# One core, two-layer hybrid decoder step: paired gate products, the first tile's output projection moved behind the prompt's scan, decay products moved to GpSimd

## The chip, the cores and the metric

One NeuronCore of a Trainium2 chip runs the whole step as one program. The metric is device time in microseconds (us); the time of a kernel is the median over its runs. A trace of one profiled execution gives the rest.

## The reference, cut to what matters

256 prompt tokens and 64 sample tokens (8 sequences of 8) go through a Mamba-2 mixer, a PEER mixer (each token fetches 128 rows of an expert table), then an attention layer and a second PEER. The change lies in the Mamba mixer and the first PEER's selection:

```python
zxbcdt = u @ w_in                      # z: gate, xbc: conv input, dt
xbc = silu(conv(xbc)); dt = softplus(dt + dt_bias); a = -exp(a_log)
# scan, chunks of 128 tokens (prompt: 2 chunks), sample: one chunk of 8 tokens in each sequence
cum = cumsum(dt * a);  decay = exp(cum_t - cum_s) for s <= t
y = (C B^T * decay) @ xdt + (C @ h) * exp(cum)
h = h * exp(cum_last) + B^T @ (tail * xdt)
y = (y + d_skip * xs) * silu(z);  y = group_rmsnorm(y) * norm_g;  h_res += y @ w_out
# PEER: q = rmsnorm(h_res) @ w_query; top 16 of 128 for each half key, top 16 of the 256 sums,
# out = sum_k gate_k * gelu(x . U[idx_k]) * V[idx_k]
```

## The kernel before, in words

Tokens lie in three tiles: tiles 0 and 1 are the prompt (128 rows each), tile 2 the samples (64 rows). All data are float32. Every engine runs one program written out in order; they meet at semaphores. PSUM has eight banks that TensorE claims round robin: `claim` waits until the bank's last reader has freed it. Weights come through a ring of four 1 MB slots (`wring`) filled by SyncE's queue in the order of `loads`; a slot is refilled when the last product that uses it is through.

The stages, in order:

1. **Gate (z).** `project_block("z", n, KD)`, four blocks of 512 columns, each in two halves of four chunks of 128; for every tile 4 matmuls of 512 columns a half (line 588). In float32 each matmul leaves two records in the trace (two passes). ScalarE makes the tanh, VectorE the rest of silu.
2. **xbc and convolution.** 32 blocks of 128 channels (line 630); VectorE does the convolution.
3. **Prompt scan.** Steps n = 0 to 15: 8 groups for tile 0, then 8 for tile 1. `decays(n)` on VectorE multiplies a mask by `da` (line 1970, 128x512), TensorE makes the segment sums from it (line 678) and C B^T (line 681), ScalarE the exp (line 1482), VectorE masks it (`mix`, lines 1983 and 1986), TensorE multiplies by xdt (line 701) and makes the new state (line 708). VectorE adds up y and gates it (lines 2132 to 2159). GpSimd makes xdt, its tailed copy and the skip term (lines 2526, 2527, 2529), two steps behind `gated`. After step 7 and step 15 the tile's rows are normalised (`scale_rows`, line 1995) and turned (`turn_rows`).
4. **Sample scan.** Steps g = 0 to 7 (n = 16 to 23). In each, TensorE turns 16 blocks of old state (`sample_turn`, line 560), makes the next step's segment sums, y, the state's part (line 659, 32 records: eight sequences times two halves of the output partitions, alternating) and the state update (line 667: four matmuls with 64 rows of contraction each, `rows = slice(64 * q, 64 * q + 64)`, 8 records). GpSimd scales the old states (line 2543, 128x1024, twice a step), VectorE adds the update (line 2103). Between these, `after_sample_turn(g)` puts the first tile's next work: output projection in two blocks (g = 0 and 1, line 588 again), norm for PEER (g = 2), queries (g = 2 to 5, line 746), scores (line 731), and on VectorE the first ten of twenty selection steps of tile 0 (`early_picks`, 3, 3, 2, 2 at g = 4 to 7; a quad of heads has five steps).
5. **Gathers.** When VectorE says `scan_over` (line 1883 after `turn_rows(2)`), GpSimd starts the expert gathers (line 2564), 1280 of 512 KB each in seven phases; VectorE multiplies every gathered `peer_u` row by the token (`dot`, line 2220), TensorE sums the `peer_v` rows (line 1103). Everything else (selection of later tiles, late output projection of tiles 1 and 2, attention) runs beside the gathers.

Of the kernel before, what the change touches and what calls it, by code (L numbers as in the profile page):

```python
# [36 lines left out]
ARENA = 31744  # L37


C_ID, C_TRI, C_STRICT, C_TRIS, C_STRICTS, C_ONES, C_BM, C_ID2, C_IOTA, C_END = 0, 128, 256, 384, 448, 512, 640, 648, 712, 728  # L40


def shape_constants():
# [12 lines left out]
    c[64:, C_BM:C_BM + 4] = k // DEC_T == 4 + np.arange(4)[None, :]  # L56
# [75 lines left out]
def build(nc, I, O, counts):  # L132
# [3 lines left out]
    with ctx:  # L136
# [123 lines left out]

        load_sent = [0]

        def load_weights(sp, upto):
            while load_sent[0] < upto:
                i = load_sent[0]
                if i >= NW:
                    sp.wait_ge(*full_at(last_user[i - NW]))
                sp.dma_start(slot_view(i), loads[i][0]).then_inc(*w_ready[i % NW].mark(by=16))
                load_sent[0] += 1
# [284 lines left out]
        def _(pe):  # L554
# [38 lines left out]
            def project(key, nblocks, kchunks):  # L593
                for n in range(nblocks):
                    project_block(key, n, kchunks)
# [11 lines left out]
            project_block("z", 0, KD)  # L607
# [6 lines left out]
            for n in range(1, 4):  # L614
                project_block("z", n, KD)
# [33 lines left out]
            def sample_states(g):  # L649
# [21 lines left out]
            def scan_front(t, g):  # L671
# [3 lines left out]
                pe.wait_ge(*dve_done.at(("seg", t, g)))  # L675
# [115 lines left out]
            for n in range(3 * GROUPS):  # L791
# [327 lines left out]
            def late():  # L1119
# [4 lines left out]
                for n in range(2):  # L1124
                    acc = {t: claim(pe, ("late_out", n, t)) for t in (1, 2)}
                    for part in range(4):
                        w = weight(pe, ("late_out", n, part), ("late_out", n, 2))
                        for t in (1, 2):
# [4 lines left out]
                            if part == 3:  # L1133
                                mm.then_inc(*full(("late_out", n, t)))
                        yield
# [23 lines left out]
            def first_select():  # L1159
                for _ in range(10):  # L1160
                    yield
# [61 lines left out]
        def _(sp):  # L1223
# [58 lines left out]
            load_state(3)  # L1282
            for g in (6, 7):
                store_final(g)
            for g in range(8):
# [4 lines left out]
                if g < 6:  # L1290
                    load_weights(sp, load_index[("out", 0, 0)] + (8, 10, 14, 16, 18, 20)[g])
# [108 lines left out]
        def _(act):  # L1400
# [28 lines left out]
            for n in range(4):  # L1429
                for t in range(3):  # L1430
                    bank = filled(act, ("z", n, t))
                    s(act.activation(z[0:ROWS[t], t, n * 512:(n + 1) * 512], bank[0:ROWS[t], :], ACT.Tanh, scale=0.5),
                      act_done, ("ztanh", n, t))
# [67 lines left out]
            def after_sample_turn(g):  # L1501

                if g == 0:
                    take_sub_keys(0)
                if g == 1:
                    square("ffn0", 0, dve_done.at(("h", "mix", 0, 0)))
                if g == 2:
                    take_turned("ffn0", 0)
                if 2 <= g < 6:
                    for b in range(4 * g - 8, 4 * g - 4):  # L1510
                        bank = filled(act, ("q", b))
                        freeing(act.activation(qT[:, b, 0:128], bank[:, 0:128], ACT.Copy), ("q", b))
                if g in (3, 4, 6):
                    take_score(0, 0, (0, 1, None, 2)[g - 3])
# [310 lines left out]
            def first_select():  # L1825
                for _ in range(10):
# [51 lines left out]
        def _(dve):  # L1878
# [47 lines left out]
            for n in range(4):  # L1926
                for t in range(3):
# [4 lines left out]
                    freeing(dve.tensor_tensor(zz, zz, bank[0:ROWS[t], :], ALU.mult), ("z", n, t))  # L1932
# [143 lines left out]
            def after_sample_turn(g):  # L2076

                if g < 2:
                    add_to_h("out", 0, 0, g)
                if g == 1:  # L2080
                    norm("ffn0", FFN_SLOT, (0,))
                if g >= 4:
                    advance(early_picks, (3, 3, 2, 2)[g - 4])

            def block_rows(g):

                if g >= 2:
                    dve.wait_ge(*full_at(("hupd", 2 * g - 3, 1)))
                s(dve.tensor_tensor(bm[:, g % 2, :, :], repeat(btok[:, 2, g * 128:(g + 1) * 128], 4),
                                    spread(cst[:, C_BM:C_BM + 4], 128), ALU.mult), dve_done, ("bm", g))  # L2090
# [16 lines left out]
            def first_picks():  # L2107
                for q in range(2):
# [3 lines left out]
            decays(0)  # L2112
# [487 lines left out]
```

## Time and profile before

| | us |
|---|---|
| median of 3 runs (2558.26 to 2571.83) | 2562.1 |
| the profiled execution's own time | 2563.79 |
| its span in the trace | 2562.0 |
| TensorE busy (70%) | 1794.2 |
| VectorE busy (61%) | 1575.0 |
| GpSimd busy (52%) | 1324.9 |
| ScalarE busy (12%) | 305.0 |

859 MB move in all, 671 MB of them by the gathers. A share of busy time is a mean over stages with different limits. The stages are read from the windows of the trace, and in a stage the wait that ends last tells what limits it. Times of one instruction on GpSimd are rough.

### The profile page before, as it was taken

To read this page: it belongs to the slowest core of one execution; us is meant where nothing else is said; L and a number is where in the kernel's file an instruction comes from. 1 tells how busy PE (TensorE), PEld (TensorE's weight loads), DVE (VectorE), ACT (ScalarE), POOL (GpSimd) and SP (SyncE) were. 2 spreads that over 40 slices of the span, in tenths; PEclk is the share of its full clock that TensorE was granted. 3 is DMA by queue.
4 is the path that set the end of the run, shared out by engine and by line. 5 is a ranking of instruction groups with operands and counts; after the bars stand their busy time and mean duration, and the time that the engine had idled before them with its cause. 6 is when DMAs were issued, how large, how long until landed. Compare 5 with 4: busy or idle time off the path is not lost.

```text
span 2562.0 us, 23629 instructions
## 1 busy us (share of the span) xinstructions
PE 1794.2 (70%) x7688; PEld 800.3 (31%) x7688; DVE 1575.0 (61%) x3823; ACT 305.0 (12%) x705; POOL 1324.9 (52%) x1480
## 2 busy tenths in 40 slices
PE   7999888676405666668778576776665658456678
PEld 4477756524400010022334223351123422001112
DVE  2288875999798656652644988768764353833321
ACT  2133322201000000010101011110012110000000
POOL 0011443255547777755665445754555363577774
PEclk9999899887756666788899786787777778699999
DMA  4232228599989999999999999999999999999997
GB/s 154 99 104 95 90 80 282 165 357 386 403 293 388 409 409 409 409 395 402 384 407 401 402 401 358 407 400 400 399 374 349 320 378 374 388 409 410 409 408 305
DMA packets 325848, 859.13 MB, mean 335 GB/s; under 512 B 26841, under 2 KB 93353, under 8 KB 325697
## 3 DMA queue, kind: packets, MB, share of 16 engines
q0 software_dynamic: 184320, 671.17, 66.7%
q1 hardware_dynamic: 141406, 186.46, 21.0%
q8 instruction: 62, 1.02, 0.2%
q14 instruction: 60, 0.49, 0.1%
HBM read 845.25 MB, written 12.17 MB: 335 GB/s over the span
## 4 chain that ended last, share of the span: by engine, by line
DMA 23%; POOL 18%; PE 12%; issue 8%; DVE 5%; SPq 3%; ACT 0%; POOLq 0%; DVEq 0%; ACTq 0%
POOL arena L2564 18%; DMA arena<-peer_v,arena 10%; DMA wring<-w_q 5%; PE banks L896 4%; PE banks L1103 3%; DMA wring<-cache_v 2%; DVE arena L2220 2%; DMA arena<-peer_u,arena 2%; SPq L1336 2%; DMA wring<-w_kv 1%; PE banks L1012 1%; SPq L1334 1%; DMA wring<-ple_w_gate 1%; DMA wring<-peer_w_query 1%; PE banks L560 1%
## 5 line engine op out<-in xcount | busy, mean ns | idle before, releaser
L2220 DVE SCALAR_TENSOR_TENSOR arena<-arena,banks 128x1024 f32<-128x1024 f32 x640 | 762.3, 1219 | 441.5 <-DMA arena<-peer_u,arena 435.7
L1103 PE MATMUL banks<-arena 128*32 128x512 f32 x2560 | 692.9, 718 | 351.6 <-DMA arena<-peer_v,arena 344.6
L2564 POOL DMA_INDIRECT arena<-peer_v,arena x640 | 607.8, 950 | 416.7 <-PE banks L1103 179.8
L2564 POOL DMA_INDIRECT arena<-peer_u,arena x640 | 606.8, 948 | 412.3 <-issue 188.7
L1103 PEld LDWEIGHTS banks<-arena 128*32 128x32 f32 x2560 | 92.5, 116 | 823.5 <-DMA arena<-peer_v,arena 655.2
L896 PE MATMUL banks<-wring,uT 128*128 128x512 f32 (+3 forms) x448 | 224.2, 650 | 67.5 <-DMA wring<-w_q 28.0
L560 PE MATMUL banks<-cst,arena 128*128 128x128 f32 (+6 forms) x498 | 78.0, 305 | 163.1 <-DVE arena L2236 83.4
L896 PEld LDWEIGHTS banks<-wring,uT 128*128 128x128 f32 (+1 forms) x448 | 80.2, 189 | 219.0 <-issue 168.1
L630 PE MATMUL banks<-uT,wring 128*128 128x320 f32 x512 | 139.1, 433 | 0.0
L560 PEld LDWEIGHTS banks<-cst,arena 128*128 128x128 f32 (+6 forms) x498 | 60.5, 156 | 213.8 <-DVE arena L2236 83.6
L588 PE MATMUL banks<-wring,uT 128*128 128x512 f32 (+1 forms) x256 | 115.8, 609 | 0.6 <-DVE arena L2103 0.6
L630 PEld LDWEIGHTS banks<-uT,wring 128*128 128x128 f32 x512 | 96.7, 190 | 40.2 <-issue 0.8
L2511 POOL COPY arena<-arena 128x3 f32<-128x3 f32 x32 | 6.0, 186 | 186.8 <-ACT arena L1458 186.8
L560 PE MATMUL banks<-cst,u 128*128 128x128 f32 (+1 forms) x256 | 43.2, 331 | 52.6 <-DVE u L1904 47.3
L834 PE MATMUL banks<-uT,wring 128*128 128x128 f32 x512 | 69.2, 293 | 9.6 <-issue 9.6
L834 PEld LDWEIGHTS banks<-uT,wring 128*128 128x128 f32 x512 | 63.9, 204 | 34.8 <-issue 34.8
L1131 PE MATMUL banks<-wring,uT 128*64 128x512 f32 (+1 forms) x128 | 62.2, 639 | 16.3 <-DMA wring<-ssm_w_out 11.9
L2027 DVE MAX8 arena<-arena 128x8 f32<-128x128 f32 (+1 forms) x208 | 60.6, 333 | 17.3 <-ACT arena L1495 16.4
L2030 DVE FIND_INDEX8 arena<-arena 128x8 uint32<-128x128 f32 (+1 forms) x208 | 67.4, 336 | 0.0
L588 PEld LDWEIGHTS banks<-wring,uT 128*128 128x128 f32 (+1 forms) x256 | 44.7, 180 | 69.4 <-issue 68.5
L2271 DVE TENSOR_SCALAR arena<-arena 128x512 f32<-128x512 f32 (+1 forms) x10 | 4.4, 437 | 92.6 <-ACT arena L1634 92.6
L560 PEld LDWEIGHTS banks<-cst,u 128*128 128x128 f32 (+1 forms) x256 | 35.6, 180 | 78.8 <-DVE u L1904 41.7
(265 smaller groups left out, 1941.6 us busy)
## 6 DMA issues: line engine op xcount, KB each, us to landing
wring<-peer_w_query SPq DMA_DIRECT2D x40, 1024.0 KB, 17.1
wring<-ssm_w_in SPq DMA_DIRECT2D x24, 1024.0 KB, 7.3
wring<-w_q SPq DMA_DIRECT2D x18, 1024.0 KB, 21.0
wring<-ssm_w_out SPq DMA_DIRECT2D x16, 1024.0 KB, 9.3
wring<-ple_w_gate SPq DMA_DIRECT2D x12, 1024.0 KB, 12.6
arena<-peer_u,arena POOLq DMA_INDIRECT x640, 12.0
arena<-peer_v,arena POOLq DMA_INDIRECT x640, 12.4
out_sample_ssm<-arena SPq DMA_DIRECT2D x16, 512.0 KB, 5.6
```

Of the source, the lines that this page charges most:

```text
L560: mm = pe.transpose(bank[0:c, col:col + r], src, ident[0:r, 0:r])
L588: mm = pe.matmul(acc[t][0:ROWS[t], 0:w.shape[2]], uT[:, kk, OFF[t]:OFF[t] + ROWS[t]], w[:, k, :], start=(kk == 0), stop=(kk == kchunks - 1))
L630: mm = pe.matmul(acc[:, 0:NTOK], w[k // 4][:, k % 4, j * 128:(j + 1) * 128], uT[:, k, :], start=(k == 0), stop=(k == KD - 1))
L834: mm = pe.matmul(bank[:, 0:R], w[k // 4][:, k % 4, (b % 4) * 128:(b % 4 + 1) * 128], uT[:, k, OFF[t]:OFF[t] + R], start=(k == 0), stop=(k ...
L896: mm = pe.matmul(bank[0:ROWS[t], 0:w.shape[2]], uT[:, kk, OFF[t]:OFF[t] + ROWS[t]], w[:, k, :], start=(kk == 0), stop=(kk == kchunks - 1))
L1103: mm = pe.matmul(sums(t, at, half), place_of(t, at), rows_buf[:, k, half * 512:(half + 1) * 512], start=at < spots(t), stop=False, skip_gr ...
L1131: mm = pe.matmul(acc[t][0:ROWS[t], :], uT[:, kk, OFF[t]:OFF[t] + ROWS[t]], w[:, k, :], start=(kk == 0), stop=(kk == 15))
L1336: sp.dma_start(last, rows[PAST - 128:, 0:2, :].rearrange("m h d -> m (h d)")).then_inc(*ready.mark(p, by=16))
L2027: step(j, dve.max(out_v[:, o], values))
L2030: step(j, dve.max_index(out_i[:, o], out_v[:, o], values))
L2220: dve.scalar_tensor_tensor(rows_buf[:, k, :], rows_buf[:, k, :], 1.0, u_now, ALU.mult, ALU.mult, accum_out=pact[:, n % 2, at:at + 1]).then ...
L2564: pool.indirect_dma_start(rows_buf[:, k, :], None, tables[kind], bass.IndirectOffsetOnAxis(ap=rows, axis=0))\
```

## The change

- **Halved gate.** For tile 2 the 512 columns of a gate block are made as two matmuls of 256 columns, whose outputs lie in the two partition halves of one bank. ScalarE and VectorE read the bank in two pieces.
- **Narrow state update.** The four matmuls of line 667 contract over 32 rows each, on four different groups of 32 rows (the four sequences that each of them needs); the mask `bm` changes to match.
- **First tile's output projection.** Its two blocks go behind step 15's scan (block 0) and into g = 0 (block 1); norm, queries, scores and selection steps all come one sample step earlier, selection has twelve early steps (3, 3, 2, 2, 2 from g = 3) and eight late ones instead of ten and ten. `part_read` frees a slot of the ring when one part of the projection has been read, for the late projection too. SyncE asks for block 1's weights before the last two stores of final prompt states.
- **Decays.** For tiles 0 and 1 the product of line 1970 is made by GpSimd, one step ahead, instead of by VectorE, two steps ahead. For tile 2 VectorE keeps it.

```diff
@@ tensor
+            def gate_block(n):
+
+                acc = {t: claim(pe, ("z", n, t)) for t in ALL}
+                for half in range(2):
+                    w = weight(pe, ("z", n, half), ("z", n, 2))
+                    for t in ALL:
+                        for k in range(4):
+                            kk = half * 4 + k
+                            for c in range(1 if t < 2 else 2):
+                                out, cols = (acc[t], w[:, k, :]) if t < 2 else \
+                                    (acc[t][64 * c:64 * c + 64, 0:256], w[:, k, 256 * c:256 * c + 256])
+                                mm = pe.matmul(out, uT[:, kk, OFF[t]:OFF[t] + ROWS[t]], cols, start=(kk == 0), stop=(kk == KD - 1))
...
-                        rows = slice(64 * q, 64 * q + 64)
+                        rows = slice(64 * i + 32 * q, 64 * i + 32 * q + 32)
...
-                pe.wait_ge(*dve_done.at(("seg", t, g)))
+                pe.wait_ge(*(pool_done if t < 2 else dve_done).at(("seg", t, g)))
...
+            def out_block(n):
+
+                bank = claim(pe, ("out", n, 0))
+                for part in range(4):
+                    pe.wait_ge(*freed(("yT", 0, part)))
+                    w = weight(pe, ("out", n, part), ("out", n, 0) if part == 3 else ("read", "out", n, part))
+                    for k in range(4):
+                        kk = part * 4 + k
+                        mm = pe.matmul(bank, uT[:, kk, 0:128], w[:, k, :], start=(kk == 0), stop=(kk == 15))
+                    mm.then_inc(*(full(("out", n, 0)) if part == 3 else part_read.mark(("read", "out", n, part))))
...
                 if g == 0:
                     turn_sub_keys(0)
-                    for q in range(4):
-                        pe.wait_ge(*freed(("yT", 0, q)))
-                if g < 2:
-                    project_block("out", g, 16, (0,))
-                if g == 2:
+                    out_block(1)
+                if g == 1:
                     pe.wait_ge(*freed(("sk", 0)))
                     norm_transposes("ffn0", (0,))
-                if 2 <= g < 6:
-                    first_queries(g - 2)
-                if g in (3, 4, 6):
-                    first_scores((0, 1, None, 2)[g - 3])
+                if 1 <= g < 5:
+                    first_queries(g - 1)
+                if g in (2, 3, 5):
+                    first_scores((0, 1, None, 2)[g - 2])
...
+                if n == 2 * GROUPS - 1:
+                    out_block(0)
@@ sync
+            load_weights(sp, load_index[("out", 0, 0)] + 8)
             for g in (6, 7):
                 store_final(g)
...
-                if g < 6:
-                    load_weights(sp, load_index[("out", 0, 0)] + (8, 10, 14, 16, 18, 20)[g])
+                if g < 5:
+                    load_weights(sp, load_index[("out", 0, 0)] + 12 + 2 * g)
@@ vector
-                if g < 2:
-                    add_to_h("out", 0, 0, g)
-                if g == 1:
+                if g == 0:
+                    add_to_h("out", 0, 0, 1)
                     norm("ffn0", FFN_SLOT, (0,))
-                if g >= 4:
-                    advance(early_picks, (3, 3, 2, 2)[g - 4])
+                if g >= 3:
+                    advance(early_picks, (3, 3, 2, 2, 2)[g - 3])
...
-            decays(0)
-            decays(1)
             mix(0)
             for n in range(3 * GROUPS):
...
-                if n + 2 < 3 * GROUPS:
+                if 2 * GROUPS <= n + 2 < 3 * GROUPS:
                     decays(n + 2)
...
+                if n == 2 * GROUPS:
+                    add_to_h("out", 0, 0, 0)
@@ gpsimd
+            decays(0)
+            decays(1)
             for n in range(3 * GROUPS):
                 t, g = divmod(n, GROUPS)
                 R, x = 128, n % 2
+                if 2 <= n + 1 < 2 * GROUPS:
+                    decays(n + 1)
                 pool.wait_ge(*freed(("cum", t)))
```

On TensorE, from the end of prompt step 15 (its last row is the turning of a final state, `cst,arena` x2) to sample step g = 1, before:

```order
L560 MATMUL banks<-cst,arena 128x128 x2
L560 MATMUL banks<-cst,u 128x128 x16
L678 MATMUL banks<-cst,arena 64x64 x4
L681 MATMUL banks<-arena 64x64
L701 MATMUL banks<-arena 64x64 x4
L659 MATMUL banks<-arena 64x128 x16
L667 MATMUL banks<-arena 128x512 x4
L560 MATMUL banks<-cst,arena 128x128 x20
L588 MATMUL banks<-wring,uT 128x512 x16
L560 MATMUL banks<-cst,arena 128x128 x16
```

and the same stretch of the changed kernel (its line 565 is the old 560, 779 the projection, 694 the old 678, 697 the old 681, 717 the old 701, 675 the old 659, 683 the old 667):

```order
L565 MATMUL banks<-cst,arena 128x128 x2
L779 MATMUL banks<-wring,uT 128x512 x16
L565 MATMUL banks<-cst,u 128x128 x16
L694 MATMUL banks<-cst,arena 64x64 x4
L697 MATMUL banks<-arena 64x64
L717 MATMUL banks<-arena 64x64 x4
L675 MATMUL banks<-arena 64x128 x16
L683 MATMUL banks<-arena 128x512 x4
L565 MATMUL banks<-cst,arena 128x128 x20
L779 MATMUL banks<-wring,uT 128x512 x16
L565 MATMUL banks<-cst,arena 128x128 x16
```

A whole projection block now stands between the end of the prompt's scan and the first turning of sample states, and the second block where the first was.

On GpSimd, the start of the prompt's scan, before (line 2526 makes xdt):

```order
L2526 TENSOR_TENSOR arena<-arena,small 128x256
L2527 TENSOR_TENSOR arena<-arena,small 128x256
L2529 TENSOR_TENSOR arena<-arena,small 128x256
L2526 TENSOR_TENSOR arena<-arena,small 128x256
L2527 TENSOR_TENSOR arena<-arena,small 128x256
```

and of the changed kernel (line 2554 is the decay product, 2572, 2573 and 2575 the three that were there):

```order
L2554 TENSOR_TENSOR arena<-cst,small 128x512 x2
L2572 TENSOR_TENSOR arena<-arena,small 128x256
L2573 TENSOR_TENSOR arena<-arena,small 128x256
L2575 TENSOR_TENSOR arena<-arena,small 128x256
L2554 TENSOR_TENSOR arena<-cst,small 128x512
L2572 TENSOR_TENSOR arena<-arena,small 128x256
```

Each prompt step gives GpSimd a fourth instruction, twice as wide as the others.

## Rows read from the trace of the kernel before

**Rows 1.** Windows by stage: us, busy us (count) of each engine, TensorE clock, DMA share, GB/s

```profile
28.00:118.00 90.00, 90.00 (x228) 34.95 (x227) 15.38 (x33) 10.98 (x19) 0.20 (x1) 1.00 0.20 71
118.00:270.00 152.00, 149.35 (x617) 108.11 (x617) 125.58 (x323) 50.99 (x124) 19.26 (x95) 1.00 0.28 97
...
444.00:516.00 72.00, 48.52 (x429) 40.61 (x429) 66.62 (x202) 15.37 (x36) 22.11 (x20) 0.82 0.52 166
516.00:760.00 244.00, 115.82 (x425) 72.97 (x423) 218.53 (x534) 14.38 (x44) 132.33 (x141) 0.73 0.98 371
760.00:2562.00 1802.00, 1232.46 (x4894) 418.69 (x4894) 1022.17 (x2467) 159.69 (x359) 1082.25 (x1139) 0.81 1.00 389
```

**Rows 2.** Timeline, gate stage, weight loads of TensorE (start us, us)

```profile
103.61 0.19 PEld L588 LDWEIGHTS banks<-wring,uT 128*64 128x64 f32 x2 [0.76 <-issue]
...
107.19 0.30 PEld L588 LDWEIGHTS banks<-wring,uT 128*128 128x128 f32 x2 [0.81 <-issue]
```

**Rows 3.** Timeline of TensorE, end of the prompt's scan and sample steps 0 and 1

```profile
346.43 1.91 PE L560 MATMUL banks<-cst,u 128*128 128x128 f32 x16
...
366.10 13.97 PE L588 MATMUL banks<-wring,uT 128*128 128x512 f32 x32 [0.61 <-DVE arena L2103]
379.90 1.91 PE L560 MATMUL banks<-cst,arena 128*128 128x128 f32 x16
...
383.32 1.97 PE L659 MATMUL banks<-arena 128*64 128x128 f32 x32
385.22 1.99 PE L667 MATMUL banks<-arena 64*128 64x512 f32 x8
387.14 13.14 PE L588 MATMUL banks<-wring,uT 128*128 128x512 f32 x30
```

**Rows 4.** Timeline of TensorE, sample steps 2, 3 and the start of 4

```profile
400.98 1.91 PE L560 MATMUL banks<-cst,u 128*128 128x128 f32 x16
...
413.80 7.38 PE L746 MATMUL banks<-uT,wring 128*128 128x128 f32 x64 [2.15 <-DVE arena L2148]
421.02 1.91 PE L560 MATMUL banks<-cst,arena 128*128 128x128 f32 x16
...
431.39 9.01 PE L746 MATMUL banks<-uT,wring 128*128 128x128 f32 x64 [2.64 <-issue]
...
441.13 1.91 PE L560 MATMUL banks<-cst,u 128*128 128x128 f32 x16
```

**Rows 5.** Timeline of VectorE, sample steps 4 to 7 and the end of the scan

```profile
444.01 0.22 DVE L1983 TENSOR_TENSOR arena<-banks,cst 64x64 f32<-64x64 f32 x1 [10.56 <-PE banks L681]
...
480.42 0.49 DVE L2027 MAX8 arena<-arena 128x8 f32<-128x128 f32 x2
...
482.90 0.22 DVE L1983 TENSOR_TENSOR arena<-banks,cst 64x64 f32<-64x64 f32 x1
...
489.59 0.49 DVE L2027 MAX8 arena<-arena 128x8 f32<-128x128 f32 x2
...
515.02 0.15 DVE L1883 COPY small<-cst 128x1 f32<-128x1 f32 x1
```

**Rows 6.** Timeline of VectorE and GpSimd, prompt scan, tile 0, then tile 1

```profile
282.00 0.61 POOL L2526 TENSOR_TENSOR arena<-arena,small 128x256 f32<-128x256 f32 x1 [3.98 <-DVE arena L2150]
282.32 0.84 DVE L1970 TENSOR_TENSOR arena<-cst,small 128x512 f32<-128x512 f32 x1
282.69 0.94 POOL L2527 TENSOR_TENSOR arena<-arena,small 128x256 f32<-128x256 f32 x1
...
283.52 0.69 DVE L1986 TENSOR_TENSOR arena<-arena 128x512 f32<-128x512 f32 x1
...
285.62 0.84 DVE L1970 TENSOR_TENSOR arena<-cst,small 128x512 f32<-128x512 f32 x1
...
328.21 0.69 DVE L1970 TENSOR_TENSOR arena<-cst,small 128x512 f32<-128x512 f32 x1
...
332.74 0.69 DVE L1970 TENSOR_TENSOR arena<-cst,small 128x512 f32<-128x512 f32 x1
```

**Rows 7.** Groups by line and shape, GpSimd, 270 to 516 us: count, busy us, mean ns, idle before

```profile
L2543 POOL TENSOR_TENSOR arena<-arena,small 128x1024 f32<-128x1024 f32 x8 | 15.7, 1961 | 55.5 <-PE banks L560 55.2
```

More of the change, by code:

```diff
@@ L266, in load_weights @@
                 if i >= NW:
-                    sp.wait_ge(*full_at(last_user[i - NW]))
+                    user = last_user[i - NW]
+                    if user is not None and user[0] == "read":
+                        sp.wait_ge(*part_read.at(user))
+                    else:
+                        sp.wait_ge(*full_at(user))
                 sp.dma_start(slot_view(i), loads[i][0]).then_inc(*w_ready[i % NW].mark(by=16))
@@ L591, in project_block @@
                             mm.then_inc(*full((key, n, t)))
-            def project(key, nblocks, kchunks):
-                for n in range(nblocks):
-                    project_block(key, n, kchunks)
+            def gate_block(n):
[9 more added lines that the diff above has]
+                                mm = pe.matmul(out, uT[:, kk, OFF[t]:OFF[t] + ROWS[t]], cols, start=(kk == 0), stop=(kk == KD - 1))
+                        if half == 1:
+                            mm.then_inc(*full(("z", n, t)))
             pe.wait_ge(*cst_in.at("cst"))
@@ L1126, in late @@
                     for part in range(4):
-                        w = weight(pe, ("late_out", n, part), ("late_out", n, 2))
+                        w = weight(pe, ("late_out", n, part), ("late_out", n, 2) if part == 3 else ("read", "late_out", n, part))
                         for t in (1, 2):
@@ L1134, in late @@
                                 mm.then_inc(*full(("late_out", n, t)))
+                            elif t == 2:
+                                mm.then_inc(*part_read.mark(("read", "late_out", n, part)))
                         yield
@@ L1159, in first_select @@
             def first_select():
-                for _ in range(10):
+                for _ in range(8):
                     yield
@@ L1431, in _ @@
                     bank = filled(act, ("z", n, t))
-                    s(act.activation(z[0:ROWS[t], t, n * 512:(n + 1) * 512], bank[0:ROWS[t], :], ACT.Tanh, scale=0.5),
-                      act_done, ("ztanh", n, t))
+                    if t < 2:
+                        s(act.activation(z[:, t, n * 512:(n + 1) * 512], bank, ACT.Tanh, scale=0.5), act_done, ("ztanh", n, t))
+                    else:
+                        for c in range(2):
+                            s(act.activation(z[0:64, 2, n * 512 + 256 * c:n * 512 + 256 * c + 256],
+                                             bank[64 * c:64 * c + 64, 0:256], ACT.Tanh, scale=0.5), act_done, ("ztanh", n, 2))
                 if n == 0:
@@ L1825, in first_select @@
             def first_select():
-                for _ in range(10):
+                for _ in range(8):
                     yield
@@ L1931, in _ @@
                     bank = filled(dve, ("z", n, t))
-                    freeing(dve.tensor_tensor(zz, zz, bank[0:ROWS[t], :], ALU.mult), ("z", n, t))
+                    if t < 2:
+                        freeing(dve.tensor_tensor(zz, zz, bank, ALU.mult), ("z", n, t))
+                    else:
+                        s(dve.tensor_tensor(zz[:, 0:256], zz[:, 0:256], bank[0:64, 0:256], ALU.mult))
+                        freeing(dve.tensor_tensor(zz[:, 256:512], zz[:, 256:512], bank[64:128, 0:256], ALU.mult), ("z", n, t))
             def conv(b):
@@ L2107, in first_picks @@
             def first_picks():
-                for q in range(2):
+                for q in range(4):
                     yield from pick_quad(0, 0, q)
             early_picks = first_picks()
-            decays(0)
-            decays(1)
             mix(0)
@@ L2443, in first_select @@
             def first_select():
-                for q in (2, 3):
-                    yield from pick_quad(0, 0, q)
+                yield from early_picks
                 yield from finish_select(0, 0)
@@ L2514, in _, with decays @@
             pool.wait_ge(vec_in.sem, 48)
+            def decays(n):
+                t, g = divmod(n, GROUPS)
+                if n >= 2:
+                    pool.wait_ge(*full_at(("seg", (n - 2) // 8, (n - 2) % 8)))
+                s(pool.tensor_tensor(seg_l[:, n % 2, :, :], repeat(strict_of(t), 4), spread(da[:, t, 4 * g:4 * g + 4], 128),
+                                     ALU.mult), pool_done, ("seg", t, g))
+            decays(0)
+            decays(1)
             for n in range(3 * GROUPS):
```

24 lines of the change are left out of this document (12 added, 12 removed).

## The prediction

> **What bounds the kernel now.** I read the windows by stage first, then the timelines of the stages that the change touches. [rows 1] split the span in four regimes. From 28 to 118 us (gate) TensorE is busy 90.0 of 90.0 us at full clock, while the DMA share is 0.20: TensorE alone sets the pace. From 118 to 270 (xbc) it is busy 149.35 of 152, with VectorE at 125.58 behind it. In the last part of the sample scan, 444 to 516, VectorE is busy 66.62 of 72: there the selection steps and the states queue on it. From 516 to the end the gathers run and the DMA share is 0.98 to 1.00; only in the first phase, 516 to 760, is VectorE also near its limit (218.53 of 244). The gathers cannot begin before the scan is over, and from there on the work is a fixed queue of bytes. So what the change is worth is how much earlier the row at 515.02 in [rows 5] comes, plus what the first phase gives.
>
> **Halved gate.** Tile 2's part of half a gate block runs from 103.61 to 107.19 [rows 2]: 3.58 us for 4 matmuls, 8 records of 512 columns. After the change it is 16 records of 256 columns on alternating halves of the output partitions. The kernel already does that in line 659: 32 records of 128 columns, alternating halves, take 385.22 - 383.32 = 1.90 us [rows 3], 0.059 us a record. Transposes of the same 128 columns that cannot pair take 1.84 us for 16 (379.90 to the row behind it), 0.115 a record. So halves do run together. 256 columns cost twice 0.059: 16 x 0.119 = 1.90 us. Saved 3.58 - 1.90 = 1.68, times 8 half blocks = 13.4 us. The stage has no other limit: weights use a fifth of the DMA and ScalarE and VectorE are busy 11 and 15 of 90 us, so their extra, narrower instructions (two for one, three for two) are hidden behind TensorE. The xbc stage starts earlier and keeps its length, since TensorE paces it. Bounds: 0 if the halves do not pair when they share their weights, 14.3 if they overlap perfectly.
>
> **Narrow state update.** The 8 records of line 667 take 387.14 - 385.22 = 1.92 us [rows 3]. Singly a record of 512 columns takes 13.14 / 30 = 0.44, and 8 would be 3.5, so two row groups already work together. Four would take about half, 1.07: 0.85 us a sample step. It counts only in steps that TensorE paces, 2 of them in the path below, and I put it there. Bounds 0 and 0.96 a step.
>
> **Projection behind the prompt's scan.** Now sample step 0 starts on TensorE at 346.43 and its projection at 366.10 [rows 3]: 19.7 us for work that takes 7.24 in the next step (379.90 to 387.14) plus 20 transposes (20 x 0.115 = 2.3). The other ten are waits for VectorE, which finishes step 15 and normalises the rows. In the new order block 0 (366.10 to 379.90, 13.8 us) fills that time. Step by step: block 0 from 346.4 to 360.2; sample step 0 takes 7.24 - 0.85, plus 2.0 because the bank claimed for line 659 is the one that holds block 0, freed only after VectorE has masked step 17 and added it: 368.6; transposes to 370.9; block 1 to 384.7. At that point the new kernel stands where the old one stands at 400.98 [rows 4], 16.3 us earlier. Then comes the norm for PEER, a serial chain that keeps its length (413.80 - 400.98), and the first queries: the next step starts at 421.02 - 16.3 = 404.7. The step from 421.02 to 441.13 costs 20.1 now. It loses the wait of 2.64 before 431.39, which was for weights that SyncE had asked for a step late (in the new order their slots are free one step ahead of the use), the 1.6 by which that query block (9.01) is slower than the one at 413.80 (7.38), and 0.85 of line 667: 15.0. So the step with the first selection starts at 419.7, and VectorE picks up 2.88 us into it, as at 444.01 - 441.13: at 422.6.
>
> From there VectorE is the limit, as it is now from 444.01 to 515.2 (71.2 us) [rows 5]. The new stretch holds one sample step more and two selection steps more. A sample step is 6.7 us (482.90 to 489.59) without its decay product, up to 9.4 with waits for GpSimd; I take 7.5. A selection step of this kind is 2.48 (480.42 to 482.90), two are 5.0. The end: 422.6 + 71.2 + 7.5 + 5.0 = 506.3 instead of 515.2, 8.9 us earlier. Bounds: 4 if the sample step costs 9.4 and step 0 loses another 3 us, 13 if the wait for the bank is absent and the step costs 6.7. SyncE is held at block 1's weights until block 0 is read, about 360; behind it stand two stores of final states and the state loads that wait for VectorE until about 368 anyway, so this costs nothing.
>
> **Decay products on GpSimd.** VectorE loses a 0.84 us (tile 0) or 0.69 us (tile 1) instruction from steps of 3.30 (282.32 to 285.62) and 4.53 us (328.21 to 332.74) [rows 6]. GpSimd gains one of a size that it never runs here. The rows at 282 show more: line 1970 starts while line 2526 runs and takes 0.84 instead of 0.69; line 2527, begun during it, takes 0.94 instead of 0.61 and ends 0.47 after it. Two-operand products of VectorE and GpSimd out of SBUF exclude each other, all but a lead-in of 0.14 us. For 512 columns on GpSimd I interpolate between 0.61 for 256 and 1.96 for 1024 [rows 6, 7]: 1.06 us, bounds 0.61 and 1.96. GpSimd's step is then 1.06 + 3 x 0.61 + four gaps of 0.08 = 3.21 plus collisions. In tile 0 VectorE's two such instructions hold the port 0.55 and 0.28 us a step, and part of that falls into GpSimd's gaps: about 0.5, so 3.7 against 3.30 now. GpSimd becomes the bound of tile 0's steps, 7 x 0.4 = 3 us lost. In tile 1 VectorE alone would be 3.8 and GpSimd with four collisions about 4.2, against 4.53: 6 x 0.33 = 2 us won. Net +1, bounds -4 and +13 (the 1.96 price: 13 steps x 0.9). The scan's end sets block 0's start, so this counts in full.
>
> The Trainium skill, "SBUF — State Buffer", section "SBUF: two separate sides", says that GpSimd and a VectorE instruction with two SBUF inputs take the shared port pair as an exclusive lock, held for the whole instruction. The rows agree that it is exclusive but not on the lead-in. By the page, tile 0's step would be 0.69 + 0.42 + 1.06 + 1.83 = 4.0 us and the sum 2 us higher.
>
> **First gather phase.** Two selection steps, 5.0 us of VectorE, leave it, and slots of the late projection are freed earlier, so that its weights come sooner. VectorE is busy 218.5 of 244 [rows 1], but DMA is also full at 0.98: I take 3 us, bounds 0 and 8. After 760 the DMA share is 1.00, and an earlier start passes through unchanged.
>
> **Sum.** -13.4 - 8.9 + 1 - 3 = -24.3 us. The profiled execution took 2563.8 (span 2562.0), 1.7 above the median. Against the median of 2562.1 that is 2538.
>
> **Rivals.**
> - *GpSimd is dear and paces the prompt's scan* (chance 0.12). For it: it is already the busier partner at the port and its spans are rough. Against it: 256 and 1024 columns lie on a line. At 1.96 a product the scan loses 13 instead of 1: 2550.
> - *The halves do not pair in the gate* (0.05), the change does not do there what it says. For it: the two share their weights, which line 659's do not. Against it: the same pattern of partitions pairs in [rows 3]. Time 2538 + 13 = 2551.
> - *More comes out of the sample stage and the first phase* (0.14): no bank wait, a step of 6.7, the phase gives its 5.0 in full and the ring a few more. Time 2538 - 4 - 5 = 2529, at most 2522.
> - *Slower than before* (0.03). One mechanism: GpSimd's product. With a price p the prompt's scan changes by about 13p - 12.6; all is lost when that reaches 24.3 + 1, at p = 2.9 us, half as much again as the row for twice its columns. Beyond that every step adds 13 for each us: 2570 at p = 3.5.
> - *The forecast* (0.66), own range 2530 to 2546.
>
> **How the numbers follow.** 0.5% of this kernel is 12.8 us, about what a measurement can tell from no change: the border is 2549.3. Of the forecast nearly all lies below it, the larger gain wholly, the two rivals near 2550 about half. Faster 0.87, same 0.10, slower 0.03. The range takes half of the dear product and of the unpaired gate and leaves out the far tails: 2525 to 2550.
>
> **What would show it.** In the profile of the changed kernel: tile 2's half block of gate 1.9 us apart and the first xbc matmul near 104.5; line 683's 8 records in about 1.07; the GpSimd product at 1.06 to 1.4 with collisions, prompt steps of 3.7 and 4.2; VectorE without the waits of some ten us for the projection, but continuous from about 409; the first gather near 495 and a first phase shorter by some 3 us. Wrong if the product on GpSimd exceeds 1.5 us, if VectorE waits for TensorE again in sample steps 3 to 6, or if the gathers, started 22 us sooner, end less than 15 us sooner.

## The result

| | us |
|---|---|
| before, median of 4 runs (2558.26 to 2572.65) | 2566.97 |
| after, median of 4 runs (2497.27 to 2507.94) | 2500.41 |
| after, the profiled execution / its span | 2497.27 / 2495.5 |

The kernel before has one run more here than in the table ahead of the prediction. The ratio is 0.9748, 95% interval 0.9707 to 0.9789: faster by 66.6 us where 24.3 were forecast, and below the predicted range. At the first gather (516.2 us in the trace before, 497.9 after) the two traces differ by 18.3 us, and up to there the forecast's own steps can be read. Of the 18.3, 2.0 us lie ahead of the gate's first matmul (27.97 against 25.94), which no part of the change touches; this start falls anywhere from 25.81 to 28.39 in the traces of the changed kernel's variants. The rest of the 66.6 arises behind the first gather, where the forecast had put 3 us and then nothing.

Windows of the changed kernel by stage, at the places that answer to [rows 1]:

```profile
26.00:104.00 78.00, 78.00 (x302) 36.88 (x301) 17.11 (x39) 12.25 (x23) 0.20 (x1) 0.98 0.26 89
104.00:253.00 149.00, 146.62 (x607) 106.14 (x605) 124.24 (x320) 50.09 (x122) 19.65 (x95) 1.00 0.27 97
444.00:498.00 54.00, 27.16 (x203) 21.60 (x199) 50.72 (x164) 7.88 (x17) 14.26 (x14) 0.67 0.42 132
498.00:740.00 242.00, 114.47 (x439) 72.02 (x438) 218.55 (x514) 15.44 (x48) 133.91 (x142) 0.73 0.97 381
740.00:2495.00 1755.00, 1203.50 (x4882) 405.88 (x4881) 1017.55 (x2454) 158.63 (x355) 1079.61 (x1138) 0.83 0.99 398
```

The last window is the surprise: the DMA share is 0.99 where [rows 1] have 1.00, but it moves 398 GB/s where they have 389. The DMA engines were busy nearly all the time in both kernels and moved more in one. 100 us in the middle of that stage, first of the kernel before, then of the changed one (same columns):

```profile
900.00:1000.00 100.00, 66.50 (x188) 9.83 (x187) 61.57 (x141) 1.66 (x4) 75.59 (x81) 0.64 1.03 409
```

```profile
900.00:1000.00 100.00, 64.62 (x160) 7.01 (x160) 67.66 (x176) 0.46 (x2) 75.59 (x81) 0.69 1.03 419
```

The page's table of queues says the same by packet. Its q0 row (packets, MB, share of the 16 engines' span), before and then after:

```profile
q0 software_dynamic: 184320, 671.17, 66.7%
```

```profile
q0 software_dynamic: 184320, 671.17, 66.5%
```

0.667 x 16 engines x 2562.0 us / 184320 packets is 0.1483 us a packet before, and 0.665 x 16 x 2495.5 / 184320 is 0.1441 after.

TensorE's timeline of the gate, its first row and the first of the next stage, before and then after:

```profile
27.97 23.95 PE L588 MATMUL banks<-wring,uT 128*128 128x512 f32 x48
...
117.83 32.57 PE L630 MATMUL banks<-uT,wring 128*128 128x320 f32 x120
```

```profile
25.94 19.50 PE L609 MATMUL banks<-wring,uT 128*128 128x512 f32 x64
...
101.18 3.23 PE L646 MATMUL banks<-uT,wring 128*128 128x320 f32 x11
```

The stage from block 0 to sample step 2 in the changed kernel, which answers to [rows 3 and 4]:

```profile
331.55 13.90 PE L779 MATMUL banks<-wring,uT 128*128 128x512 f32 x32
345.28 1.91 PE L565 MATMUL banks<-cst,u 128*128 128x128 f32 x16
...
352.53 3.68 PE L675 MATMUL banks<-arena 128*64 128x128 f32 x32 [3.87 <-DVE h L2045]
356.14 1.43 PE L683 MATMUL banks<-arena 32*128 32x512 f32 x8
...
374.55 1.91 PE L565 MATMUL banks<-cst,arena 128*128 128x128 f32 x16
...
394.60 1.91 PE L565 MATMUL banks<-cst,u 128*128 128x128 f32 x16
...
400.34 1.14 PE L683 MATMUL banks<-arena 32*128 32x512 f32 x8
```

Prompt scan, tile 0, GpSimd and VectorE (answers to [rows 6]), line 2022 being the old 1986; then the end of the sample scan on VectorE, whose row before is the last of [rows 5]:

```profile
277.25 1.04 POOL L2554 TENSOR_TENSOR arena<-cst,small 128x512 f32<-128x512 f32 x1
277.35 1.49 DVE L2022 TENSOR_TENSOR arena<-arena 128x512 f32<-128x512 f32 x1 [0.55 <-ACT arena L1515]
...
281.00 1.04 POOL L2554 TENSOR_TENSOR arena<-cst,small 128x512 f32<-128x512 f32 x1
281.09 1.49 DVE L2022 TENSOR_TENSOR arena<-arena 128x512 f32<-128x512 f32 x1 [0.55 <-ACT arena L1515]
```

```profile
496.71 0.15 DVE L1915 COPY small<-cst 128x1 f32<-128x1 f32 x1
```

### The profile page after: what moved, and what is told of

Read it like the earlier page. It is cut to its first block, busy times and chain, and to the rows that moved or that the text cites. A ratio compares the mean times of both kernels' runs of the same rounds, so it can differ in the third digit from the quotient of the medians.

```text
span 2495.5 us, 23767 instructions
## 1 busy us (share of the span) xinstructions
PE 1745.5 (70%) x7752; PEld 786.5 (32%) x7752; DVE 1569.1 (63%) x3811; ACT 305.7 (12%) x709; POOL 1339.7 (54%) x1496
## 3 DMA queue, kind: packets, MB, share of 16 engines
q0 software_dynamic: 184320, 671.17, 66.5%
## 4 chain that ended last, share of the span: by engine, by line
POOL 21%; DMA 17%; PE 12%; issue 9%; DVE 8%; SPq 4%; ACT 0%; POOLq 0%; DVEq 0%; ACTq 0%
POOL arena L2610 21%; DMA arena<-peer_v,arena 7%; PE banks L922 4%; DMA wring<-w_q 4%; PE banks L1129 3%; DVE arena L2255 3%; DMA wring<-cache_v 2%; SPq L1365 2%; PE banks L1038 1%; SPq L1363 1%; DMA wring<-peer_w_query 1%; DMA wring<-w_kv 1%; PE banks L860 1%; PE banks L565 1%; DMA arena<-peer_u,arena 1%
## 5 line engine op out<-in xcount | busy, mean ns | idle before, releaser
L1129 PE MATMUL banks<-arena 128*32 128x512 f32 x2560 | 678.8, 714 | 334.8 <-DMA arena<-peer_v,arena 328.3
L922 PEld LDWEIGHTS banks<-wring,uT 128*128 128x128 f32 (+1 forms) x448 | 80.1, 189 | 209.1 <-issue 164.7
L609 PE MATMUL banks<-wring,uT 128*128 128x512 f32 (+1 forms) x256 | 73.2, 499 | 0.0
L1038 PE MATMUL banks<-wring,arena 128*64 128x128 f32 x208 | 28.0, 299 | 41.6 <-DMA wring<-cache_v 40.2
## 6 DMA issues: line engine op xcount, KB each, us to landing
wring<-ple_w_gate SPq DMA_DIRECT2D x12, 1024.0 KB, 11.8
```

The source lines that it names most:

```text
L609: mm = pe.matmul(out, uT[:, kk, OFF[t]:OFF[t] + ROWS[t]], cols, start=(kk == 0), stop=(kk == KD - 1))
L922: mm = pe.matmul(bank[0:ROWS[t], 0:w.shape[2]], uT[:, kk, OFF[t]:OFF[t] + ROWS[t]], w[:, k, :], start=(kk == 0), stop=(kk == kchunks - 1))
L1038: pe.matmul(bank[rows, 0:128], pts[:, b, rows], cache[:, 1, 13 * b2 + b, :], start=(b == 0), stop=False)
L1129: mm = pe.matmul(sums(t, at, half), place_of(t, at), rows_buf[:, k, half * 512:(half + 1) * 512], start=at < spots(t), stop=False, skip_gr ...
```

## The experiments

### Where the rate of the gathers comes from

Two lines of the full diff that the excerpt ahead of the prediction leaves out, shortened:

```diff
-ARENA = 31744
+ARENA = 31736
-C_ID, ..., C_IOTA, C_END = ..., 712, 728
+C_ID, ..., C_IOTA, C_SEQ, C_END = ..., 712, 728, 736
```

Theory A: they add 8 columns to the constants (for the new mask), and the tensors behind them, the gathers' row buffers among them, move by 32 bytes, and that makes the gathers faster. Theory B: the new order, or the earlier start, makes the gathers faster.

**e1_before_shift32.**

```diff
-ARENA = 31744
+ARENA = 31736
-... C_IOTA, C_END = ... 712, 728
+... C_IOTA, C_END = ... 712, 736
```

> The kernel before, with nothing changed but 8 unused columns behind the constants, so that every tensor behind them in SBUF lies 32 bytes further, as in the changed kernel (2944 bytes from the first tensor's start, a multiple of 64, in place of 2912). Theory A (the place of the buffers is what speeds the gathers: 0.1483 us of queue time per packet before, 0.1441 after): the rate of the stretch 900 to 1000 rises from 409 to about 420 GB/s, the time falls by 40 to 50 us to 2515 to 2525, ratio about 0.982. Theory B (the order of weights and picks of the change, or an earlier start, is what speeds them): 409 GB/s, time unchanged, ratio 1.00.

**e2_after_shift32**: the changed kernel with C_END 744 and ARENA 31728.

> The changed kernel, with 8 more unused columns behind the constants (2976 bytes, no multiple of 64, 32 bytes past one again). Theory A: the rate in saturated stretches falls from 419 to about 409 GB/s and the time rises from 2500 to 2540 to 2550, ratio to the kernel before about 0.990, as the prediction had it. Theory B: 2500, ratio 0.975.

**e3_before_shift160**: the kernel before with C_END 768 and ARENA 31704.

> The kernel before with 40 unused columns behind the constants: every later tensor starts at a multiple of 1024 bytes (3072). Theory A in the form 'a multiple of 64 is enough': the same time as with 8 columns, 2515 to 2525. In the form 'the larger the multiple the better' (a multiple of 256 or 512 saves a further piece of each row): below 2515. Theory B: 2562.

**e5_before_rows_only.**

```diff
-        rows_buf = area(SEL + 5888, PSLOTS, D)
+        rows_buf = area(SEL + 5896, PSLOTS, D)
```

> The kernel before with one thing changed: the ring of row buffers that the gathers write (14 rows of 4096 bytes in the arena) lies 8 columns (32 bytes) further; everything else stays where it was. With the whole memory behind the constants moved by 32 bytes the time fell from 2566 to 2512. The buffers' first byte is then at a multiple of 256 (and was 32 bytes short of one). If it is the gathers' own rows that count: the same 2512, rate 420 GB/s in 900:1000. If it is the weights, the caches or the operands of the engines: 2566 and 409 GB/s. In between if both.

**e7_after_rows512**: the changed kernel with `SEL + 5952`.

> The changed kernel with the row buffers 256 bytes further, at a multiple of 512 bytes in place of an odd multiple of 256. If only the multiple of 256 counts: 2500, 419 GB/s as in the changed kernel. If a larger multiple saves more: below 2490.

**e12_before_rows_at_64**: the kernel before with `SEL + 5912`.

> The kernel before with only the row buffers moved, by 96 bytes, to 64 bytes past a multiple of 256. So far the rows were at 409 GB/s with their first byte 224, 32 and 128 past such a multiple, and at 419 to 420 at 0. If each row of 4096 bytes is cut at multiples of 256, only 0 is fast: 409 GB/s, 2566. If a multiple of 64 is enough: 419 GB/s, 2512 to 2520. If the bytes from the boundary to the row's first byte are what costs (64 against 224): a rate between, 415 to 418, and 2530 to 2540.

The tensors between the first one and the row buffers take 162912 bytes of a partition before and 162944 after. I took the first tensor to begin at byte 8320, as the compiled program has it; no run or trace here shows that byte. With it the row buffers begin at 171232 before and at 171264 after. Rates are those of 900:1000. Each ratio goes by the runs of the kernel before that were measured beside it (medians 2565.68 to 2569.64).

| kernel | first byte past a multiple of 256 | GB/s | median us | ratio to before, 95% |
|---|---|---|---|---|
| before | 224 | 409 | 2566 | 1 |
| e2 (after, moved) | 32 | 409 | 2556.24 | 0.9970 [0.9956, 0.9983] |
| e12 | 64 | 409 | 2570.06 | 0.9999 [0.9984, 1.0014] |
| e3 | 128 | 409 | 2565.82 | 0.9990 [0.9971, 1.0009] |
| e1 | 0 | 420 | 2511.96 | 0.9793 [0.9772, 0.9814] |
| e5 (row buffers alone) | 0 | 419 | 2520.41 | 0.9825 [0.9796, 0.9854] |
| after | 0 | 419 | 2500.41 | 0.9748 [0.9707, 0.9789] |
| e7 (a multiple of 512) | 0 | 419 | 2501.61 | 0.9759 [0.9723, 0.9794] |

The windows of e1, e12 and e2, in this order:

```profile
900.00:1000.00 100.00, 65.41 (x192) 9.24 (x192) 64.20 (x149) 1.66 (x4) 75.52 (x80) 0.70 1.03 420
```

```profile
900.00:1000.00 100.00, 63.97 (x188) 9.19 (x188) 62.77 (x145) 1.66 (x4) 75.50 (x80) 0.69 1.03 409
```

```profile
900.00:1000.00 100.00, 64.13 (x188) 9.92 (x188) 64.07 (x158) 1.89 (x5) 75.63 (x81) 0.67 1.03 409
```

Theory A stands and B falls. 32 bytes and no other edit gave the kernel before 54 us (e1; the whole change gave 66.6), and took 56 from the changed one (e2). The row buffers alone give 45 (e5); e1 and e5 are 8 us apart with intervals that overlap, so whether the place of the other tensors adds a little stays open. e1 came out 3 us below its range and e2 6 above its own, for which the next section has a reason. e3 came out where B had put it and against both forms of A in its expectation. Only e5, e7 and e12 explain it. The form "a multiple of 64 is enough" was wrong: e12 and e3 lie at such multiples and are slow. The form "the larger, the better" e3 did not test, since its row buffers came to 128 past a multiple of 256; e7, 256 bytes further than the changed kernel, shows no further gain.

What of this rests on runs alone: against the fast place of e1 and e5, rows that lie 32 bytes lower or 32, 64 or 128 bytes higher are slow, and in the changed kernel 256 bytes higher are fast again. So the places repeat at 256 bytes and at nothing shorter that these runs tried. That the fast place is a multiple of 256 itself needs the byte 8320.

The window 900:1000 tells less than it seems to of how fast the rows in place can go. In both traces GpSimd starts a gather of 524288 bytes every 1.24 us there, which asks for about 422 GB/s. In the kernel before the landings fall behind, from 10.6 us after the issue in 900:925 to 13.8 in 975:1000; in the changed kernel they stay at 7.2 to 7.7. The rates of 1100:1400, 397 before and 413 after, tell the same difference where fewer gathers are started.

The Trainium skill, "DMA: Bandwidth & Descriptors", section "How a descriptor splits into AXI transactions", says that a transfer is cut into pieces that start at multiples of 256 bytes, and of a read that the bytes between the boundary and its first byte cost beats as well. An estimate from that page: a row of 4096 bytes has 16 pieces in place and 17, or 6% more, out of place. For the writes here the first half agrees in kind: all four places off the multiple cost alike. The second does not show, as 32, 64, 128 and 224 bytes give one rate of 409 GB/s. The measured cost is 2.9% a packet (0.1483 against 0.1441), not 6%. That the pieces are the cause is argued from the places; no row shows a piece.

### Where the written change was lost on the way

e2 has the whole written change and the old rate, and it gained 10 us, not 24. Its gathers start 15.8 us before those of the kernel before (500.4 against 516.2) and keep at least that lead until TensorE waits for the cached values of the last pair of samples in the second attention. TensorE's waits for cached values, in the kernel before and in e2 (start us, us, ..., idle before):

```profile
2000.52 5.76 PE L1012 MATMUL banks<-wring,arena 128*64 128x128 f32 x26 [20.33 <-DMA wring<-cache_v]
2031.91 5.43 PE L1012 MATMUL banks<-wring,arena 128*64 128x128 f32 x26 [5.12 <-DMA wring<-cache_v]
2067.56 4.69 PE L1012 MATMUL banks<-wring,arena 128*64 128x128 f32 x26 [8.88 <-DMA wring<-cache_v]
```

```profile
1982.54 5.78 PE L1038 MATMUL banks<-wring,arena 128*64 128x128 f32 x26 [20.17 <-DMA wring<-cache_v]
2012.21 4.69 PE L1038 MATMUL banks<-wring,arena 128*64 128x128 f32 x26 [2.63 <-DMA wring<-cache_v]
2059.66 4.94 PE L1038 MATMUL banks<-wring,arena 128*64 128x128 f32 x26 [21.39 <-DMA wring<-cache_v]
```

The third wait is 12.5 us longer, and the lead falls from 19.7 us at the second row (2031.91 to 2012.21) to 7.9 at the third. SyncE's queue tells what is late. The last three issues of these values in the kernel before, then in e2 (start us, us that the issue holds the queue):

```profile
2043.53 0.58 SPq L1332 DMA_DIRECT2D wring<-cache_v  x1
2044.15 1.98 SPq L1334 DMA_DIRECT2D wring<-cache_v  x1
2046.18 4.23 SPq L1336 DMA_DIRECT2D wring<-cache_v  x1
```

```profile
2027.64 1.29 SPq L1361 DMA_DIRECT2D wring<-cache_v  x1
2028.97 5.32 SPq L1363 DMA_DIRECT2D wring<-cache_v  x1
2034.33 10.81 SPq L1365 DMA_DIRECT2D wring<-cache_v  x1
```

The same transfers take 6.8 us to issue in one and 17.4 in the other. GpSimd's gathers stop for TensorE meanwhile, 22.95 us long in e2 (to 2071.18) and 10.17 in the kernel before, and in 2040:2080 of e2 the DMA share is 0.69 (0.01 in 2060:2070): the stage that was taken for full runs dry. The changed kernel has the long form too:

```profile
2007.28 5.45 PE L1038 MATMUL banks<-wring,arena 128*64 128x128 f32 x26 [21.31 <-DMA wring<-cache_v]
```

The load is asked for when the values of the pair before have been read, as it goes into the same memory. To test it, the last pair's values were sent to other memory that is free earlier, that of the keys of the pair before, once these are turned:

**e6_after_values_early**; e10 is the same edit on the kernel before, e11 on e2. Two of its lines, shortened; the readers and a signal of its own follow them:

```diff
-    dst = key_halves[p % 2][b2] if w == 0 else cache[:, 1, 13 * b2:13 * b2 + 13, :]
+    dst = key_halves[p % 2][b2] if w == 0 else key_halves[0][b2] if p == 3 else cache[:, 1, ...]
-    sp.wait_ge(*full_at(("so", p - 1)))
+    sp.wait_ge(*full_at(("so", p - 1) if p < 3 else ("kc", 2, 6)))
     load_cache(p, 1)
```

> The changed kernel, with the cached values of the last pair of samples loaded into the memory of the pair before's keys, as soon as these are turned, and no longer after the pair before's values are read. The theory (a start about 17 us earlier is passed on until gather 958, where TensorE waits 21.3 us for these values because their issue is stuck behind the pair before's in a full queue, and 8.9 us in the kernel before): this wait goes, gather 959 follows 958 within 2 us and the time falls by 10 to 20 us, to 2480 to 2490. The rival (the wait moves to another landing in the same saturated queue, as the bytes are the same): 2495 to 2505.

> The kernel before with the last pair's cached values loaded early, as in the run of the changed kernel that gained 9. In the kernel before TensorE waits 8.9 us for them, not 21.3. If the early load gains what the wait was above what is left of it there (5.5): 3 to 4 us, 2562 or so, ratio 0.998 to 1.00. If it gains the same 10 as in the changed kernel, the loss had nothing to do with the difference of the two: 2556.

> The changed kernel with its row buffers out of place as in the kernel before (32 bytes past a multiple of 256) and with the last pair's values loaded early. Against the kernel before with the early values this leaves the whole written change and nothing else, with neither the place nor the wait for the values between them. By the theory the start of the gathers, 16 to 18 us earlier, is then passed on whole: 2543 to 2547, 15 to 19 below that run. By the rival (the saturated stage eats a part of any earlier start, wherever): 2550 to 2555, 6 to 10 below it.

Measured: e6 2491.4 us, ratio 0.9689 [0.9657, 0.9721], 9 us below the changed kernel and 10 below e7, which was measured beside it and is as fast as the changed kernel; e10 2564.51, 0.9987 [0.9974, 1.0001]; e11 2543.34, 0.9907 [0.9879, 0.9936]. e6 missed its range of 2480 to 2490 by 1.4, and the rival's by more. e10 gained 2.8 where 3 to 4 were expected, with an interval that just reaches no change, and e11 lies in its range, though 2 us further below e10 than expected. In it the wait of 21.31 is 5.54, though gathers still stop for 12.39 us there, so not within the 2 us that I had expected:

```profile
1996.82 5.48 PE L1042 MATMUL banks<-u,arena 128*64 128x128 f32 x26 [5.54 <-DMA wring<-cache_v]
```

e11 against e10 is the written change with rows out of place in both and the waits nearly alike (7.35 and 9.35 us): 21.2 us by the medians. First and last gathers, e10 then e11:

```profile
L2568 POOL DMA_INDIRECT arena<-peer_u,arena x640: 932/937/2212, 515.3 to 2432.6; - x160
L2568 POOL DMA_INDIRECT arena<-peer_v,arena x640: 932/937/2207, 751.5 to 2535.1; - x160
```

```profile
L2614 POOL DMA_INDIRECT arena<-peer_u,arena x640: 932/937/2212, 497.7 to 2408.7; - x160
L2614 POOL DMA_INDIRECT arena<-peer_v,arena x640: 932/937/2207, 730.0 to 2510.9; - x160
```

The lead is 17.6 us at the first gather (0.6 of it from the start of the gate), 21.5 when the second phase begins and 24.2 at the last. The 24.2 flatters: e11's profiled execution is the fastest of its four, 2.3 us below their median, and e10's is 0.7 above its own. So the saturated stage does pass an earlier start on; it was this one wait that took it back. It took 11.3 us in e2 (21.2 less the 9.9 that e2 gained), and 6.2 in the changed kernel, if the 9.0 that e6 gained are counted less the 2.8 that the same edit gave the kernel before. The rival of a stage that eats a part anywhere falls.

Why the wait is long is open. The lead may do it: pair 3 is asked for 28.5 us behind pair 2 in e2, 24.9 in the changed kernel and 31.1 in the kernel before, among full gathers. But the wait is no property of the changed order alone. In traces with the old order it is 3.01 (e5), 6.14 (e1), 8.88 (before), 11.91 (e3) and 16.63 us (e12), where pair 3 is asked for 30.1 to 31.1 us behind pair 2; with the new order it is 10.48 in e4 and 19.67 to 21.39 in the changed kernel, e2, e7, e8 and e9. e12, 2.9 us ahead of the kernel before at the second row, is 4.2 behind it at the third.

### The parts of the written change

**e4_after_whole_gate**: `gate_block(n)` replaced by `project_block("z", n, KD)`, and its readers on ScalarE and VectorE with it.

> The changed kernel with the gate's projection of the sample tile undone: 512 columns on 64 rows, as before. The traces of the two kernels put 14.6 us on the gate (89.86 against 75.24 us from its first matmul to the next stage's). If this passes through to the end unchanged, the time is 2515, ratio 0.980; if the saturated gather stage takes part of it up, less; if it is doubled there, up to 2530. Its gather rate should stay at 419 GB/s by theory A and by theory B.

2510.82 us, 0.9807 [0.9766, 0.9848]: 10.4 us above the changed kernel. Its gate takes 89.25 us (first matmul to first xbc matmul) against 75.24, 14.0 for the pairing. 3.6 us of these do not arrive at the end; its wait for the last pair's values is 10.48 us and not 21.31.

**e8_after_decays_back**: the 16 products on VectorE again.

> The changed kernel with the 16 products of the prompt's scan back on VectorE, as in the kernel before. The traces put +1.7 us on the whole prompt scan (76.3 to 78.0), so 2499 if the scan's end passes on; the prediction had put +1 on it. The rival (GpSimd's own relief of VectorE, 0.756 us per step, gave more than the trace of the scan tells): slower than 2500 by up to 10, 2510.

2504.43 us, 0.9741 [0.9710, 0.9771], not to be told from the changed kernel. Its prompt scan takes 77.7 us from the first matmul of the cumulative sums (253.19) to block 0, whose row is below, and 78.3 in the changed kernel (253.27 to 331.55). The move to GpSimd costs 0.6 us there, and nothing that the medians could show:

```profile
330.91 13.90 PE L779 MATMUL banks<-wring,uT 128*128 128x512 f32 x32
```

**e9_after_wide_update**, its main line; the mask goes back with it:

```diff
-                        rows = slice(64 * i + 32 * q, 64 * i + 32 * q + 32)
+                        rows = slice(64 * q, 64 * q + 64)
```

> The changed kernel with the state update of the samples as before: each record on 64 rows in place of 32, so two groups of rows at work and not four. The prediction put 0.85 us per step on the narrow update, 6.8 us for the 8 steps, all in the path: by it 2507, and the scan's end 6.8 us later than 498.1. The rival, from the trace of the changed kernel (VectorE without a gap from 412 us on): only the steps before 412 are TensorE's, so 1 to 3 us at the scan's end and 2501 to 2504.

2505.78 us, 0.9755 [0.9719, 0.9790], not to be told from the changed kernel by the medians. Block 0 starts 2.5 us later than there (334.08), as the gate did (28.39 against 25.94), which the edit does not touch; the first copy behind the scan (line 2278) comes 5.3 later (503.42 against 498.12). That leaves 2.8 us for the narrow update. The expectation has the prediction wrong here: 6.8 would be eight steps at 0.85, but the prediction put the 0.85 into two steps only, 1.7 us. The records themselves are nearly as priced: 1.99 us for 8 with 64 rows, 1.14 with 32 (1.07 forecast).

## Why the prediction was wrong

**The step that failed** is "After 760 the DMA share is 1.00, and an earlier start passes through unchanged". A full queue was taken for a fixed time. Its bytes are fixed, its rate is not: [rows 1] gave 389 GB/s, and the diff changed what that number rests on. `C_END` and `ARENA` stand in the full diff. I left both out of the excerpt and costed neither. This is worth 54 to 56 us (e1, e2). The second half of the step failed too: e2, with the old rate, started its gathers 15.8 us sooner and ended 9.9 sooner by the medians, less than the 15 that the prediction had named as a sign of being wrong, since the share does not stay at 1.00 (0.69 in 2040:2080). That took 6 to 11 us. The parts add up: e1 and e2, each against the kernel before, give -54.1 - 9.9 = -64.0, and -66.6 were measured.

**The sum of the written change** came near, 24.3 forecast and 21.2 by the medians of e10 and e11, but not term by term: its largest miss is the sample stage, and the gate and the time behind the first gather gave more than they were put at. At the first gather 16 to 17 us were there without the chance start of the gate (18.3 - 2.0 and 17.6 - 0.6), and 21.3 were forecast. Its terms:

- *Gate*: -13.4 forecast, -14.6 between the traces (89.86 to 75.24 us, just outside the bound of 14.3), 14.0 by e4. Right, as was the reading that halves pair.
- *Decays*: +1 forecast, +1.8 between the traces (76.5 to 78.3), +0.6 by e8. The product takes 1.04 (1.06 forecast), tile 0's step 3.75 (3.7) and tile 1's 4.27 (4.2). What was not foreseen is who pays: line 2022 takes 1.49 in place of 0.69, because it starts 0.1 us behind GpSimd's product. That this costs nothing, as GpSimd paces these steps, is read from the steps' lengths and not tested alone.
- *Sample stage*: -8.9 forecast. From the end of the prompt's scan to the copy behind the sample scan (346.43 to 515.02 before, 331.55 to 496.71 after) the traces give -3.4. This term is mis-sized, nearly all of it in sample step 0: step 1 comes 43.0 us after block 0 started, 38.3 forecast. The bank that holds block 0 costs 3.87 us before line 675 (2.0 forecast), and that group takes 3.68 in place of 1.97. The granted clock is 0.50 in 352.5:356, the 1.2 GHz level, after TensorE had run nothing for those 3.87 us. The prediction priced step 0 by step 1, where TensorE did not wait; the trace before had the slow form in step 0 already, also at a clock of 0.50 (356:360; its row stands below this list). The next two steps are as forecast (20.05 and 14.95 against 20.0 and 15.0). The narrow update, put at 1.7 us, gave 2.8 (e9).
- *First gather phase*: -3 forecast. The start of the second phase is 3.9 further ahead than the first gather in e11 against e10, but only 1.8 in e2 against the kernel before. In the changed kernel it is 7.5, and in e1, with the rate alone, 4.3.

```profile
356.08 3.68 PE L659 MATMUL banks<-arena 128*64 128x128 f32 x32 [1.22 <-ACT arena L1526]
```

Of the rivals, the dear product on GpSimd, the unpaired halves and the slower kernel did not occur. "More comes out of the sample stage and the first phase" lies on the side where the time came out, by luck: its sample stage without a wait for the bank is refuted by the 3.87 us, and the time came from the rate.

## What to carry to other kernels

Work out the first byte of every buffer that a bound queue writes, before and after, even where a diff seems only to resize a constant: off the place that repeats every 256 bytes, these rows of 4096 cost 2.9%. Where a stage is a full queue, its rate is a term of the sum like any other. An earlier start passes such a stage on, but a transfer that shares the queue and is asked for just in time can take it back, and asking for it earlier, into other memory, gives most of it back. And a group of instructions is priced by the row of its own place in the old trace, with its clock, not by the tidiest row of its kind.

## What was not expected of the hardware

- With the gathered rows of 4096 bytes 32, 64, 128 or 224 bytes past the place that repeats every 256, 900:1000 moves 409 GB/s, and 419 to 420 on it. The median from issue to landing there is 11.8 us before and 7.3 after, as the landings fall behind the issues in the one and hardly in the other.
- One DMA issue on SyncE's queue can hold it for 0.58 us or for 10.81 (line 1365 in e2, at 1993.99 and 2034.33). The long ones stand behind other issues among full gathers; that the queue had no room for them is argued.
- A VectorE product that starts 0.1 us behind a GpSimd product of 1.04 us takes 1.49 in place of 0.69.
